# Splitting 640 tokens as 512 + 128 instead of 320 + 320 in the dense products

## The reference, cut to what matters

```python
D_MODEL, SEQ, DEC_SEQ, DEPTH, D_FF = 1024, 128, 512, 4, 4096

# mixer of layers 0 and 3: r, k, v = xr @ w_rkv[0], xk @ w_rkv[1], xv @ w_rkv[2];  ... ; y @ w_o
# mixer of layer 1:        qkv = h @ w_qkv  (1024 x 1536);  block attention;  o @ w_o
# mixer of layer 2:        proj = h @ w_in  (1024 x 4096 and gates);  gated delta rule;  o @ w_o

def squared_relu_mlp(h, w_fc1, w_fc2):
    return jnp.square(jax.nn.relu(h @ w_fc1)) @ w_fc2

def deepnorm_residual(x, delta, gate, g, b):
    return layer_norm(DEEPNORM_ALPHA * x + gate * delta, g, b)
```

## Time and profile before

| | |
|---|---|
| three runs | 8619.19, 8628.42, 8630.40 us |
| median | 8628.42 us |
| the profiled execution, first to last instruction (span) | 8614.4 us |
| TensorE matmuls busy | 6895.8 us, 80% of the span |
| TensorE weight loads busy | 5819.8 us, 68% |
| VectorE busy | 4241.4 us, 49% |
| ScalarE busy | 1628.0 us, 19% |

### The profile page before, as it was taken

One profiled execution on the slowest core, in us unless ns is written; L12 is line 12 of the kernel. 1 busy time (PEld: TensorE's weight loads), 2 busy tenths in 40 slices (PEclk: granted clock), 3 DMA queues, 4 the chain that ended last, 5 costly groups with the idle time before them and its releaser, 6 DMA issues. The chain is left out here.

```text
span 8614.4 us, 112116 instructions
## 1 busy us (share of the span) xinstructions
PE 6895.8 (80%) x44860; PEld 5819.8 (68%) x44860; DVE 4241.4 (49%) x7492; ACT 1628.0 (19%) x2928; POOL 290.5 (3%) x260
## 2 busy tenths in 40 slices
PE   7788888888798677798945676699678887888698
PEld 1666666666698555697944565599566666666698
DVE  0446666666434422434156666433546666666433
ACT  0211111111222122323221111222211111111322
POOL 0000000000000000000000000000000000000000
PEclk9899999999899777899977787799888888888899
DMA  6221111110221200221311000121110000000121
GB/s 244 78 76 38 38 38 39 38 38 32 73 73 47 77 16 16 74 78 49 113 51 37 25 19 20 64 70 60 65 50 9 9 9 9 9 9 3 68 78 56
DMA packets 96935, 429.11 MB, mean 50 GB/s; under 512 B 16041, under 2 KB 26537, under 8 KB 64873
## 3 DMA queue, kind: packets, MB, share of 16 engines
q1 hardware_dynamic: 83248, 392.92, 12.9%
q10 hardware_dynamic: 13248, 30.15, 0.9%
HBM read 374.03 MB, written 49.26 MB: 49 GB/s over the span
## 5 line engine op out<-in xcount | busy, mean ns | idle before, releaser
L343 PE MATMUL bank<-src_hi,ring_hi 128*128 128x320 f32 x4032 | 936.6, 314 | 358.9 <-DVE ring_lo L335 354.9
L343 PE MATMUL bank<-src_lo,ring_hi 128*128 128x320 f32 x4032 | 933.3, 313 | 7.4 <-issue 7.4
L343 PEld LDWEIGHTS bank<-src_hi,ring_hi 128*128 128x128 f32 x4032 | 688.4, 192 | 362.8 <-issue 358.2
L343 PE MATMUL bank<-src_hi,ring_lo 128*128 128x320 f32 x4032 | 932.5, 313 | 0.0
L343 PEld LDWEIGHTS bank<-src_lo,ring_hi 128*128 128x128 f32 x4032 | 688.6, 192 | 7.8 <-issue 7.8
L343 PEld LDWEIGHTS bank<-src_hi,ring_lo 128*128 128x128 f32 x4032 | 687.6, 191 | 0.0
L335 DVE TENSOR_TENSOR ring_lo<-ring,ring_hi 128x2048 fp32r<-128x2048 f32 x190 | 434.9, 2289 | 508.6 <-ACT ring_hi L331 507.7
L735 PE MATMUL bank<-xx,y 128*128 128x128 f32 x3200 | 522.6, 286 | 75.5 <-DVE y L768 56.3
L779 DVE TENSOR_TENSOR xx<-bank,xx 128x512 f32<-128x512 f32 x600 | 414.7, 691 | 289.0 <-PE bank L739 289.0
L768 DVE TENSOR_TENSOR y<-bank,const 128x256 f32<-128x256 f32 x1000 | 416.1, 421 | 283.3 <-PE bank L727 277.4
L727 PE MATMUL bank<-xx,lt 128*128 128x128 f32 x3200 | 501.5, 288 | 26.1 <-DVE xx L779 26.1
(11 more groups left out here) (354 smaller groups left out, 11469.4 us busy)
## 6 DMA issues: line engine op xcount, KB each, us to landing
ring<-w_mlp SPq DMA_DIRECT2D x128, 1024.0 KB, 4.8
mod_ring<-w_mod SPq DMA_DIRECT2D x24, 2048.0 KB, 7.7
mod_slab<-w_mod SPq DMA_DIRECT2D x24, 2048.0 KB, 7.6
ring<-rw_wrkv SPq DMA_DIRECT2D x24, 1024.0 KB, 4.7
ring<-dn_win SPq DMA_DIRECT2D x16, 1024.0 KB, 5.2
rkv<-stage ACTq DMA_DIRECT2D x48, 320.0 KB, 2.2
rkv<-rkv SPq DMA_DIRECT2D x48, 320.0 KB
rows<-dn_rows SPq DMA_DIRECT2D x8, 1920.0 KB, 6.8
```

The costliest lines, as they stand in the source:

```text
L343: last = self.nc.tensor.matmul(acc[h][:, 0:HALF], wt[:, n % 2, k, m * P:(m + 1) * P], x[:, k, h * HALF:(h + 1) * HALF], start=first and q ...
```

## The change

The two halves of 320 tokens become the 512 latent and the 128 context tokens. The number of matmuls, of weight loads and of evacuations stays as it is, and so do their order, their waits and the total of columns. The first matmul of every pair grows from 320 to 512 columns and now fills its PSUM bank; the second shrinks from 320 to 128. The same holds for the two copies out of PSUM.

```diff
-HALF = T // 2
+TOKENS = (S_LAT, S_CTX)

         for q, (wt, x) in enumerate(parts):
-            for h in range(2):
-                last = self.nc.tensor.matmul(acc[h][:, 0:HALF], wt[:, n % 2, k, m * P:(m + 1) * P],
-                                             x[:, k, h * HALF:(h + 1) * HALF], start=first and q == 0, stop=end and q == 2)
+            for h, cols in enumerate(TOKENS):
+                last = self.nc.tensor.matmul(acc[h][:, 0:cols.stop - cols.start], wt[:, n % 2, k, m * P:(m + 1) * P],
+                                             x[:, k, cols], start=first and q == 0, stop=end and q == 2)
...
-                            for h in range(2):
-                                last = nc.scalar.copy(row[:, h * HALF:(h + 1) * HALF], acc[u][h][:, 0:HALF])
+                            for h, cols in enumerate(TOKENS):
+                                last = nc.scalar.copy(row[:, cols], acc[u][h][:, 0:cols.stop - cols.start])
...
-                            for h in range(2):
-                                last = nc.scalar.activation(stage[:, u % 2, h * HALF:(h + 1) * HALF],
-                                                            acc[u % UNITS][h][:, 0:HALF], ACT.Relu if u < NB else ACT.Copy)
+                            for h, cols in enumerate(TOKENS):
+                                last = nc.scalar.activation(stage[:, u % 2, cols],
+                                                            acc[u % UNITS][h][:, 0:cols.stop - cols.start],
+                                                            ACT.Relu if u < NB else ACT.Copy)
```

## The result

The changed kernel takes 9050.63 us (median of three, 9047.65 to 9058.06), the kernel before 8628.42 us: a ratio of 1.0495, with a 95% interval of 1.0476 to 1.0514. That is 422 us more; the forecast was 414 us more, 9042 us. The profiled execution's span grew from 8614.4 to 9045.9 us.

A forecast was written before the change was run, and what follows sets the result against it. TensorE's stream was taken as the bound. Pairs lengthened by 397 us at the high clock and 17 us at the low make 414 us; 9028 us of span becomes 9042 on the median, range 8924 to 9236.

The forecast's parts named there:

- The bound: Dense phases: TensorE's instruction stream is the limit, and what it gains or loses arrives at the end one for one.
- the sum: All dense products: 8960 pairs x 44.3 ns plus 160 pairs at half clock x 106 ns, 414 us more.
- The floor: Dense products: a matmul cannot start sooner than about 110 ns after the one before it started; short step 111 ns.
- The reading of the three records after a wait: First loads and matmul of L343 after a wait: 107 ns from a load's start until its matmul could run.
- The long matmul: The 512-column matmul of each pair: 226.7 ns at the high clock, bounds 216 to 234.7.
- The 13.4 ns: Time of a 320-column matmul beside its columns at the high clock, taken unchanged for 512 columns.
- The low clock: Start of each phase at half clock: a pair takes 640 ns against 534, 160 pairs, 17 us in all.
- Copies and clock: The two copies out of PSUM counted as 0, at most 2 us uncovered; no drop expected in TensorE's clock.
- Nothing changes: Dense products: loads run further ahead and overhead is fixed, so a pair stays 293.4 ns; 8628 us, chance 0.09.
- faster: Dense products: overhead falls to 2.5 ns and no load binds; pair 271.7 ns, 198 us less, 8430; chance 0.04.
- Rival (c): Dense products: today's 146.7 ns is already the pace of loads; pair 373.4 ns, +80 ns, 9371 us; chance 0.10.
- (d): Short matmul runs at a quarter of the rate, 213 ns; pair 440 ns, about +1340 us, 9970; chance 0.04.

## Why the prediction was right

- **The bound.** TensorE's stream sets each dense phase and everything it loses arrives at the end: shown by 431.7 us more in the 16 phases and 431.5 us more of span.
- **The size, and some luck.** The span grew by 431.5 us where the sum said 414, so the sum was 18 us short. The time came out only 9 us off, because I had set the median 14.0 us above the span, "for what lies around the span". In every later run of the kernel before, time and span of the same execution differ by 1.7 to 1.9 us; by that, most of the 14.0 is the difference between the profiled execution and the median one. The changed kernel's median lies 4.7 us above its profiled span. The two errors partly cancel.
- **The floor.** The step that decided, 110 ns from start to start behind the short matmul, came out at 108 (forecast 111). Halving the load that lies behind the short matmul removed the loss, halving the other one did nothing. The reading of the three records after a wait was what made it safe for the short type.
- **The long matmul.** Forecast 226.7 ns, measured 232. The 13.4 ns do not stay fixed: medians of the steps give 4 ns beside 128 columns (58 in the run with the short load), 10 beside 256, 13 beside 320, 16 beside 384, 18 beside 448, 19 beside 512 (16 in the run whose long matmuls have half the weights). So the bound that had them grow in full proportion (234.7) was nearer than the constant that I chose. The constant was 5 ns too low and the short step 3 ns too high, which leaves the pair 3 ns too low, 340.5 against 337.7: 3 x 8960 = 27 us is the main miss of the sum. Against it stands that the low clock has about 145 pairs instead of my 160.
- **The low clock.** 640 ns a pair was forecast and 640 measured, from 430 and 210 ns where I had 427 and 213.
- **What was read wrongly.** The scan's and norm's float32 matmuls were counted as one record each; they are two. The four loads of the earlier trace rows belong to two matmuls, and so do the four records of the earlier trace rows. The argument went by spacing of records, so it held, but "a float32 matmul of 128 columns takes 112 ns" is wrong: it takes two such steps. Nor does give the time beside the columns, the "2.5 for one pass": a load of about 110 ns lies under the same step of 112. And "every load seen begins with, not before, the preceding matmul" is true of the dense products, of the changed kernel's too, but not of the whole trace: in the scan's matmuls that write only one half of the output columns, four loads, of 0.14 us at most, begin within 0.20 - 0.14 = 0.06 us, and the fourth begins 94 ns before the matmul of the third:

```profile
694.03 0.20 PEld L1203 LDWEIGHTS bank<-state,const 128*64 128x64 f32 x4
```

- **Copies and clock.** Priced at nothing: outside the products the time is the same to 0.2 us, and the MLP's granted clock is 0.99 in both.
- **The rivals.** "Nothing changes" and "faster" both need a 128-column matmul that can be followed sooner than 110 ns. The run with the short load shows that the array itself could (58 ns); what it can't do is load 128 weight columns of this type in that time. The Trainium skill's "TensorE: Matmul & The Clock Gate", section "Back-to-back issue gap", lists 134 cycles for 128 columns, 56 ns at 2.4 GHz, and the 58 ns are near that. The same section says that in a stream with loads both count, and gives about 81 ns for 128 columns and 131 for 512; this trace has 108 and 232, and the measurement decides. Had the table been used without the load beside it, the sign would have been wrong. Rival (c), a floor of 147 ns, and (d), 213 ns, fall by the measured 108.

No version here beats both kernels with the whole computation: 384 + 256 ties with 320 + 320, and what went faster left out part of the weights.

## What to carry to other kernels

When every matmul carries its own weights, a matmul that is shorter than the load of the next one's weights costs that load. Split moving columns so that each part covers it: here the point lies between 224 and 256 columns for 128 columns of fp32r weights. The exposed load is that of the successor, so it is read from the spacing of loads, and tested by shortening that one load alone. Whether two parts are equal does not matter above the floor.

## What the runs showed of the hardware that I had not expected

- Behind a matmul that is shorter, a load of 128 weight columns of fp32r sets a step of 108 ns at 2.4 GHz and 210 at 1.2 GHz. At 2.4 GHz one of float32 does the same (110 ns), while a transpose's takes 57. That is about two cycles for each column of weights, though the matmul needs one for each moving column.
- A load of half the columns under a matmul that covers it changes nothing (ratio 1.0003, 0.9993 to 1.0012).
- A float32 matmul appears as two loads and two matmuls in the trace: 9120 of them added 9120 records of each kind (53,980 against 44,860).
- The time of an fp32r matmul beside one cycle per column grows with its columns, from 4 ns at 128 to 19 at 512, and was 21 at 416 next to a matmul of 224. The cause is open.
